# A decoder layer's feed-forward loop: a fifth chunk pair by Strassen's products, low parts by adding DMAs, seven slots

## The reference, cut to what matters

```python
f = rmsnorm(h, g_ffn)
h = h + (silu(f @ w_gate) * (f @ w_up)) @ w_down
```

## Time and profile before

| | |
|---|---|
| median of 3 runs | 1168.04 us (1167.95 to 1168.8) |
| the profiled execution | 1168.28 us, of which 1166.5 us are the span of the profile |
| PE, DVE, ACT, POOL busy | 1152.6, 944.9, 631.3, 141.5 us |
| granted TensorE clock | 0.998 of full speed |
| HBM read | 220.63 MB, 191 GB/s over the span |

### The profile page before, as it was taken

One profiled execution on the slowest core, in us unless ns is written; L12 is line 12 of the kernel. 1 busy time (PEld: TensorE's weight loads), 2 busy tenths in 40 slices (PEclk: granted clock), 3 DMA queues, 4 the chain that ended last, 5 costly groups with the idle time before them and its releaser, 6 DMA issues.

```text
span 1166.5 us, 16361 instructions
## 1 busy us (share of the span) xinstructions
PE 1152.6 (99%) x5618; PEld 969.2 (83%) x5618; DVE 944.9 (81%) x1266; ACT 631.3 (54%) x811; POOL 141.5 (12%) x90
## 2 busy tenths in 40 slices
PE   9999999999999999999999999999999999999996
PEld 8889989988888787888888888888888888888886
DVE  6589767767777999988989898988989898947674
ACT  6544365466465564646456564647364555637552
POOL 0212443336124300000000000000000000000111
PEclk9999999999999999999999999999999999999999
DMA  9655555444655575564747474745647374754541
GB/s 345 211 182 179 182 180 179 154 174 146 214 177 158 173 254 191 210 211 146 259 135 257 140 251 143 254 164 200 209 154 258 129 266 136 247 200 159 198 163 72
DMA packets 113120, 223.38 MB, mean 191 GB/s; under 512 B 5193, under 2 KB 6417, under 8 KB 112816
## 3 DMA queue, kind: packets, MB, share of 16 engines
q1 hardware_dynamic: 112608, 222.08, 56.2%
q10 hardware_dynamic: 464, 0.66, 0.2%
HBM read 220.63 MB, written 2.10 MB: 191 GB/s over the span
## 4 chain that ended last, share of the span: by engine, by line
PE 91%; DVE 3%; issue 2%; POOL 1%; ACT 1%; POOLq 0%; DVEq 0%; ACTq 0%
PE ps L1421 14%; PE ps L1423 14%; PE ps L1422 14%; PE ps L1624 12%; PE ps L1625 12%; PE ps L1626 12%; PE ps L1455 3%; PE ps L1454 3%; PE ps L1453 3%; PE ps L1463 2%; DVE w_lo L963 1%; PE ps L1619 1%; PE ps L1617 1%; PE ps L1618 1%; PE ps L1430 0%
## 5 line engine op out<-in xcount | busy, mean ns | idle before, releaser
L668 ACT ACTIVATE w_hi<-w_raw 128x1024 fp32r<-128x1024 f32 (+1 forms) x286 | 291.2, 1028 | 273.3 <-PE ps L1423 156.0
L963 DVE TENSOR_TENSOR w_lo<-w_raw,w_hi 128x1024 fp32r<-128x1024 f32 x250 | 301.9, 1220 | 121.0 <-ACT w_hi L668 120.7
L1421 PE MATMUL ps<-w_hi,oT_hi 128*128 128x512 f32 x320 | 125.8, 393 | 0.0
L1422 PE MATMUL ps<-w_lo,oT_hi 128*128 128x512 f32 x320 | 124.7, 390 | 0.0
L1423 PE MATMUL ps<-w_hi,oT_lo 128*128 128x512 f32 x320 | 124.7, 390 | 0.0
L1421 PE MATMUL ps<-w_hi,nT_hi 128*128 128x512 f32 x280 | 111.4, 398 | 0.0
L1423 PE MATMUL ps<-w_hi,nT_lo 128*128 128x512 f32 x280 | 109.1, 390 | 0.0
L1422 PE MATMUL ps<-w_lo,nT_hi 128*128 128x512 f32 x280 | 109.0, 389 | 0.0
L576 POOL TENSOR_TENSOR w_lo<-w_raw,w_hi 128x1024 fp32r<-128x1024 f32 x36 | 86.7, 2408 | 181.8 <-ACT w_hi L668 181.8
L1019 DVE SCALAR_TENSOR_TENSOR ps<-arena,taps,ps 128x256 f32<-128x256 f32 x232 | 94.6, 481 | 0.2 <-ACT ps L789 0.2
L1624 PE MATMUL ps<-w_hi,nT_hi 128*128 128x512 f32 x220 | 86.9, 395 | 1.4 <-DVE w_lo L963 1.4
(11 more groups left out here) (278 smaller groups left out, 2598.5 us busy)
## 6 DMA issues: line engine op xcount, KB each, us to landing
w_raw<-in_w_gate SPq DMA_DIRECT2D x88, 512.0 KB, 3.9
w_raw<-in_w_up SPq DMA_DIRECT2D x88, 512.0 KB, 4.8
w_raw<-in_w_down SPq DMA_DIRECT2D x44, 1024.0 KB, 5.1
w_raw<-in_w_in SPq DMA_DIRECT2D x32, 1024.0 KB, 5.1
w_raw<-in_w_out SPq DMA_DIRECT2D x16, 1024.0 KB, 5.0
w_raw<-in_w_pgate SPq DMA_DIRECT2D x16, 1024.0 KB, 5.1
w_raw<-in_w_in SPq DMA_DIRECT2D x14, 512.0 KB, 10.5
w_raw<-in_w_ple SPq DMA_DIRECT2D x2, 1024.0 KB, 7.4
```

Of the source, the lines that this page charges most:

```text
L668: nc.scalar.activation(tiles_of(m)[0], source_of(m), ACT.Copy).then_inc(hi_ready, 1)
L963: nc.vector.tensor_tensor(lo, source_of(m), hi.bitcast(F32), ALU.subtract).then_inc(lo_ready, 1)
L1421: nc.tensor.matmul(banks[t][:, :], x_hi[:, k, rows], hi[:, k], start=start, stop=False)
L1422: nc.tensor.matmul(banks[t][:, :], x_hi[:, k, rows], lo[:, k], start=False, stop=False)
```

## The change

- The kinds become PPSSSSSP: the fifth pair takes seven products too. A pass has 26 units of pairs and 8 of the down product, `PER_LOOP` = 34, `DOWN_AT` = 26.
- The fifth pair's sums of x take the rows of `oT_hi` and `oT_lo` that were a slot. Seven slots are left, and their numbering starts anew with each pass (`slot_back`). `align` moves ahead of `w_extra`.
- For the down columns 1, 2 and 3 DVE makes no low part. Behind the high part ACT writes a second `F32R` copy of the raw weights into the low tile, with `scale=-1.0`, and POOL issues a DMA that adds `w_down` from HBM to this tile (`accum_op=ALU.add`). SP reloads the raw buffer of such a column when this copy is done.
- The sums of x ahead of the loop move from POOL to DVE, two pairs in one instruction, and start one unit earlier; the first weight sums move behind the first swish.

```diff
-QUAD_KINDS = "PPSSPSSP"
+QUAD_KINDS = "PPSSSSSP"
-LOOP_SLOTS = 8
+LOOP_SLOTS = 7
+DMA_COLUMNS = (1, 2, 3)
-RB1_AT = FFN0 + 6
+RB1_AT = FFN0 + 5
-S_AT = {i: RB1_AT + 4 + n for n, i in enumerate(S_QUADS)}
+S_GROUPS = [S_QUADS[n:n + 2] for n in range(0, len(S_QUADS), 2)]
+X_SUMS_AT = [NORMAL_AT[group[-1]] for group in S_GROUPS]
+S_AT = [NORMAL_AT[group[-1]] + 1 for group in S_GROUPS]
...
+def by_dma(m):
+    return in_loop(m) and loop_unit(m)[0] == "D" and loop_unit(m)[1] in DMA_COLUMNS
...
+        sb("align", [P, 8])
         w_extra = sb("w_extra", [P, 2, 4, NP], F32R)
-        sb("align", [P, 8])
...
-                n = (m - LOOP0) % LOOP_SLOTS
+                n = (m - LOOP0) % PER_LOOP % LOOP_SLOTS
                 if n == 4:
-                    return tuple(o[:, 12:16].rearrange("p (k a) t -> p k (a t)", k=2) for o in (oT_hi, oT_lo))
-                if n == 5:
                     return w_more[:, 0:2], w_more[:, 2:4]
-                if n >= 6:
-                    return w_extra[:, n - 6, 0:2], w_extra[:, n - 6, 2:4]
+                if n > 4:
+                    return w_extra[:, n - 5, 0:2], w_extra[:, n - 5, 2:4]
                 return w_hi[:, n], w_lo[:, n]
...
+        def slot_back(m):
+            j = (m - LOOP0) % PER_LOOP
+            if j >= LOOP_SLOTS:
+                return LOOP_SLOTS
+            return PER_LOOP - max(k for k in range(PER_LOOP) if k % LOOP_SLOTS == j) + j
...
             elif in_loop(m) and m >= LOOP0 + LOOP_SLOTS:
-                engine.wait_ge(half_done, m - LOOP_SLOTS + 1 + PER_LOOP * it)
+                engine.wait_ge(half_done, m - slot_back(m) + 1 + PER_LOOP * it)
...
             def down_split(c, it):
+                if c in DMA_COLUMNS:
+                    sp.wait_ge(minus_hi_ready, 2 * (DMA_COLUMNS.index(c) + 1) + 2 * len(DMA_COLUMNS) * it)
+                    return
                 sp.wait_ge(lo_ready, lo_count(LOOP0 + DOWN_AT + 2 * c + 1, it))
...
-            for n, i in enumerate(S_QUADS):
-                x_sums(n, i)
+            done = 0
+            for m in filter(by_dma, range(LOOP0, PLE0)):
+                _, c, k = loop_unit(m)
+                rows = 4 * ((m - LOOP0) // PER_LOOP) + 2 * k
+                done += 1
+                pool.wait_ge(minus_hi_ready, done)
+                nc.gpsimd.dma_start(slot_of(m)[1], w_down_v[:, rows:rows + 2, c * NP:(c + 1) * NP], accum_op=ALU.add).then_inc(lo_by_dma[c, k], 16)
...
                 nc.scalar.activation(tiles_of(m)[0], source_of(m), ACT.Copy).then_inc(hi_ready, 1)
+                if by_dma(m):
+                    nc.scalar.activation(tiles_of(m)[1], source_of(m), ACT.Copy, scale=-1.0).then_inc(minus_hi_ready, 1)
...
             def split_lo(m, it=0):
+                if by_dma(m):
+                    return
...
+            def x_sums(g):
+                first, end = S_GROUPS[g][0], S_GROUPS[g][-1] + 1
+                x = w_sum[:, first:end].rearrange("p n (k t) -> p n k t", k=2)
+                a11, a12, a21, a22 = x[:, :, 0, 0:P], x[:, :, 1, 0:P], x[:, :, 0, P:T], x[:, :, 1, P:T]
+                out_s = s_raw(g)
+                ve.wait_ge(x_normal, end)
+                nc.vector.tensor_tensor(out_s[:, :, 0], a21, a22, ALU.add).then_inc(s_step, 1)
+                nc.vector.tensor_tensor(out_s[:, :, 2], a11, a21, ALU.subtract).then_inc(s_step, 1)
...
-                for i in S_QUADS:
-                    ahead = QUAD_AT[i] - LOOP_SLOTS
-                    if ahead < 0 and m - LOOP0 in (ahead, ahead + 1):
-                        weight_sums(m - LOOP0 - ahead, 0, i)
...
+                if m in (LOOP0 + SLOTS, LOOP0 + SLOTS + 1):
+                    weight_sums(m - LOOP0 - SLOTS, 0, S_FIRST)
                 split_lo(m)
...
             def arrived(m, it=0):
+                if by_dma(m):
+                    pe.wait_ge(hi_ready, m + 1 + PER_LOOP * it)
+                    pe.wait_ge(lo_by_dma[loop_unit(m)[1:]], 16 + 16 * it)
+                    return
                 pe.wait_ge(lo_ready_pool if by_pool(m) else lo_ready, lo_count(m, it))
```

More of the change, by code:

```diff
@@ L134, in by_pool @@
     return 8 <= m < POOL_UNTIL and (m % 4 == 3 or m % 2 == 1 and m >= POOL_HALF)
+def by_dma(m):
+    return in_loop(m) and loop_unit(m)[0] == "D" and loop_unit(m)[1] in DMA_COLUMNS
 def lo_count(m, it=0):
-    return sum(by_pool(i) == by_pool(m) for i in range(m + 1)) + PER_LOOP * it
+    return sum(by_pool(i) == by_pool(m) and not by_dma(i) for i in range(m + 1)) + (PER_LOOP - 2 * len(DMA_COLUMNS)) * it
 def taps_done(g, m):
@@ L270, in x_norm, with s_raw, s_parts @@
         def x_norm(i):
[L272 to L281, removed]
+            return w_sum[:, i].rearrange("p (k t) -> p k t", k=2)
+        def s_raw(g):
+            first = 2 * (g % 2)
+            return sums[:, first:first + len(S_GROUPS[g])].rearrange("p n (s t) -> p n s t", s=4)
+        def s_parts(n, count=1):
+            return tuple(o[:, 4 + 2 * n:4 + 2 * (n + count)].rearrange("p (n a) (b t) -> p n (a b) t", a=2, b=2)
+                         for o in (oT_hi, oT_lo))
         def a_parts(i):
@@ L374, in hybrid_decoder_layer @@
         w_sum_ready = sem("w_sum_ready")
+        minus_hi_ready = sem("minus_hi_ready")
+        lo_by_dma = {(c, k): sem(f"lo_by_dma{c}{k}") for c in DMA_COLUMNS for k in range(2)}
         x_joined, x_normal, s_step, s_hi_ready, s_ready = sem("x_joined"), sem("x_normal"), sem("s_step"), sem("s_hi_ready"), sem("s_ready")
@@ L583, in join_x @@
                                         ALU.add).then_inc(x_joined, 1)
[L585 to L597, removed]
             for m in filter(by_pool, range(POOL_UNTIL)):
@@ L856, in a_hi, with s_hi @@
                 nc.scalar.activation(a_parts(i)[0], x_norm(i), ACT.Copy).then_inc(a_hi_ready, 1)
-            def s_hi(n):
-                sc.wait_ge(s_step, 4 * n + 4)
-                nc.scalar.activation(s_parts(n)[0], s_raw(n), ACT.Copy).then_inc(s_hi_ready, 1)
+            def s_hi(g):
+                sc.wait_ge(s_step, 4 * g + 4)
+                nc.scalar.activation(s_parts(2 * g, len(S_GROUPS[g]))[0], s_raw(g), ACT.Copy).then_inc(s_hi_ready, 1)
             def sigmoid_gate(c):
@@ L876, in _ @@
                         a_hi(i)
-                for n, i in enumerate(S_QUADS):
-                    if m == S_AT[i]:
-                        s_hi(n)
+                for g in range(len(S_GROUPS)):
+                    if m == S_AT[g]:
+                        s_hi(g)
                 split_hi(m + AHEAD)
@@ L1217, in weight_sums @@
                         ve.wait_ge(a_ready, 4)
-                        ve.wait_ge(s_step, 4 * len([q for q in S_QUADS if q < 4]))
+                        ve.wait_ge(s_step, 4 * len([g for g in S_GROUPS if g[0] < 4]))
                     nc.vector.tensor_tensor(w_sum[:, 0:2], raw[:, 1:3], raw[:, 0:2], ALU.subtract).then_inc(w_sum_ready, 1)
@@ L1244, in _ @@
                         normalise(i)
+                for g in range(len(S_GROUPS)):
+                    if m == X_SUMS_AT[g]:
+                        x_sums(g)
                 if m == LOOP0 - 1:
@@ L1251, in _ @@
                         a_lo(i)
-                for n, i in enumerate(S_QUADS):
-                    if m == S_AT[i]:
-                        s_lo(n)
-                for i in S_QUADS:
-                    ahead = QUAD_AT[i] - LOOP_SLOTS
-                    if ahead < 0 and m - LOOP0 in (ahead, ahead + 1):
-                        weight_sums(m - LOOP0 - ahead, 0, i)
+                for g in range(len(S_GROUPS)):
+                    if m == S_AT[g]:
+                        s_lo(g)
                 if not by_pool(m + AHEAD) and m < LOOP0 - 1:
@@ L1640, in seven_products @@
                 s_hi, s_lo = s_parts(S_QUADS.index(i))
-                s1, s2, s3, s4 = ((s_hi[:, k], s_lo[:, k]) for k in range(4))
+                s1, s2, s3, s4 = ((s_hi[:, 0, k], s_lo[:, 0, k]) for k in range(4))
                 first, last = i == S_FIRST, i == S_LAST
                 pe.wait_ge(a_ready, i + 1)
-                pe.wait_ge(s_ready, S_QUADS.index(i) + 1)
+                pe.wait_ge(s_ready, S_QUADS.index(i) // 2 + 1)
                 arrived(at, it)
```

14 lines of the change are left out of this document (9 added, 5 removed).

## The result

The changed kernel takes 1258.14 us (median of 4 runs, 1257.44 to 1258.62) against 1168.25 for the kernel before in the same comparison: a ratio of 1.0767, 95% interval 1.075 to 1.0784. The forecast was 1217, its range 1186 to 1255. The direction was right and the size was not: 90 us more instead of 49, and 3 us beyond the range. TensorE's granted clock is 0.997 in the profiled execution and 0.998 in the one of before, so the clock has no part in this.

A forecast was written before the change was run, and what follows sets the result against it. TensorE, busy 99% of the span, bounds the kernel. A pass: 64.02 - 1.18 + 3 x 1.03 + 1.2 + 1.7 = 68.8 us; in all +48.8, so 1217 us, 4.2% slower, range 1186 to 1255.

The forecast's parts named there:

- fewer and closer matmuls: TensorE in each pass: three matmuls fewer (0.68 us) and 69 at aligned spacing (0.50 us), together 1.18 us saved.
- the pairs' waits: Five seven-product pairs in a row: TensorE waits for VectorE's late splits 0.17, 0.57 and 0.46, 1.2 us a pass.
- the first pass: First loop pass: VectorE, fuller and with later weight sums, is late; today's 1.65 us loss doubles, adding 1.6 us.
- ACT's copies of P1, P5: Before the first down column: ScalarE's copies queue behind eleven activations, are ready at 32.1, and TensorE waits 1.7 us a pass.
- three release waits a pass: End of pass: split and down-panel additions end 3.71 us after a 2.72 us unit began; TensorE waits 1.03 us, three times.
- adding DMAs: GpSimd's queue, down columns 1 to 3: each takes 9.6 us, just hidden under 10.3 or more, so they cost nothing.
- Engine time is no limit: DMA engines over a pass: six adding transfers, doubled, take 18.6 us on top of 37 in some 69, so they fit.
- Rival B: Adding DMAs late by slow descriptors or two fetches: first 5.0 us late each pass, 50 in all, 1267 us; chance 0.14.
- the alignment: Moving `align` ahead of `w_extra` brings 69 matmuls a pass from 0.2338 to 0.2265 us, saving 0.50 us a pass.
- Rival A: Only the end-of-pass waits occur; the 1.2 and 1.7 us margins in the pairs and ScalarE's queue vanish: 1188 us; chance 0.14.
- Rival C: Faster: the end-of-pass release chain takes below 2.72 us, no longer than a unit, and margins vanish: 1156 us; chance 0.09.
- The relief on DVE: Six low parts of 1.14 us leave VectorE at steps 21 to 26, where it is otherwise idle or combining: nothing gained in the pairs.

The follow-up runs named there:

- the kernels with GpSimd: Changed kernel without adding DMAs or copies by -1, additions early, GpSimd subtracting for six down units: 1186.38 us; also for one unit of three pairs: 1219.9 us.

## Why the prediction was right and wrong

The 90 us, each term by the runs that differ in it alone, beside the forecast's:

| term | forecast | measured | from |
|---|---|---|---|
| fewer and closer matmuls, the pairs' waits, the first pass | +1.8 | +8.4 | no DMAs, additions and copies earlier |
| ACT's copies of P1, P5 | +17 | +17.7 | copies earlier |
| three release waits a pass | +30 | +39.8 | additions earlier |
| adding DMAs | 0 | +24.0 | DMAs left out |
| sum | +49 | +89.9 | |

The measured terms add up in this order of removal; in another the shares of the last two would differ, as the run with the DMAs in place and the additions earlier shows.

**The step that failed** is "Engine time is no limit: ... six a pass, doubled, are 18.6 us on top of 37 in some 69". Its terms were good: an adding transfer takes 2.87 us of the 16 engines against 1.67 plain, 1.72 times, six of them 17.2 us. What was wrong is the 69. The six fall into one third of the pass, and SP's loads for the next pass fall into the same third. The queues of the window over the six units in the kernel after show both (packets, MB, share of 16 engines):

```profile
q0 software_dynamic: 1318, 2.53, 65.0%
q1 hardware_dynamic: 1653, 3.18, 44.3%
```

109% together, over 21 us. The kernel without the adding DMAs shows the room that there was, in the 12 us ahead of the stage and in the stage:

```profile
643.00:655.00 12.00, 10.52 (x47) 8.40 (x46) 7.66 (x11) 12.00 (x15) 0.00 (x0) 1.00 0.87 315
655.00:671.50 16.50, 14.20 (x62) 11.13 (x61) 9.68 (x12) 6.07 (x7) 0.00 (x0) 1.00 0.50 167
```

Half of 16.5 us and 0.13 of 12 are some 10 us of engine time, and 17 came. With the engines full, the first transfer of a pass (second to ninth) lands some 9.4 us after its issue, within the 9.6 taken, but the others after 11.3 to 13.8, each 4.0 us behind the one ahead. Rival B, DMAs late at 1267, had the place, the sign and the point from which it decides (10.3 us), and was given 0.14. It erred in the form: it charged one lateness of 5.0 us a pass, but what comes is a rate. The first DMA is in time, and the five behind it are each late, 0.8 to 1.3 us at a time, 5.5 in a pass; and since PE is then held anyway, the release waits vanish into it. A pass gets 1.8 us longer by the DMAs (72.3 against 70.5), the first one 3.9, and the last stretch 5.5: there the two loads of `w_ple` stand behind adding DMAs, land in 11.3 us, ACT waits 6.65 for them, and PE 5.20 behind ACT and DVE. 8 x 1.83 + 3.9 + 5.5 make the 24.0. That last wait was in no step.

The Trainium skill (Collectives: The Full Stack, The bandwidth ceiling) has two sources read where there is a reduction, and so half the rate; the runs show 1.72 times the engine time. The Trainium skill's fit (DMA: Bandwidth & Descriptors, Anatomy of one DMA) gives 3.2 us for one such transfer by itself; among the others it took 8.9 plain and 11.7 adding. The nearest to a transfer by itself is the first one of the last pass, beside which SP's loads run out 2.5 us after its issue: it lands in 5.7 us adding and in 4.4 plain, so here the measurement is above the fit.

**A term mis-sized:** the release wait. Mechanism, places and number of waits were as forecast (28 of 29; all three go when the additions move). Its price was taken from the earlier trace rows at 1.03 us; it is 1.41. Of the 0.38 between, 0.09 is the chain on ACT and DVE, 0.18 the two further waits that PE passes before it starts and 0.11 the late second matmul behind it. The same 0.11 makes the pairs' three waits 1.34 + 0.33 = 1.67 us where the forecast has 1.2, and this 0.47, ten times, is most of the 6.6 us by which the first line of the table is off. The first pass is the rest: without DMAs and with both moved it is 4.7 us over the others (69.29 against 64.55), where 1.65 + 1.6 was taken.

**Right:** the waits inside the pairs (0.57, 0.44 and 0.33 against 0.17, 0.57 and 0.46), in all 1.34 for 1.2; ACT's late copies (1.64 against 1.7); the alignment, 5.2 us measured for 5.0; no change ahead of the loop; the passes without DMAs 70.5 against 68.8. **Rival A** (these margins vanish) fell: both waits are there, within 0.15 us of their sizes. **Rival C** (faster) fell: the chain is 4.02, not below 2.72. The relief on DVE was said to give nothing back, and it does not: with the additions early DVE makes all low parts at no cost. GpSimd's 60 issues took 1.2 us each (one 1.36), so nothing held it while it wrote descriptors.

Four things stay open. Why the first pass waits more: its timeline shows DVE behind in every pair, with three waits of 0.8 and eight of 0.2 to 0.4 where a later pass has three in all, but no run changed the order ahead of it. The adding DMA's 1.72 is measured at one size of packet and from HBM to SBUF only. No run moved SP's loads out of the stage, so that the adding DMAs would be in time without them is argued from the last pass alone. And the kernels with GpSimd show that contended operations stand still, but only 6.2 of the 9 us of the first are seen as waits of PE.

## What to carry to other kernels

Work out engine time of DMAs over the stage in which they are issued, with what the other queues load in that stage, not over the pass; a queue that loads ahead is at its fullest just where its buffers come free. Before moving work to an engine or a queue "that has nothing else to do", look whether the one relieved was late at all: here, without the DMAs, the order of the down additions and of two copies cost 57 us, and DVE's six low parts nothing. Remember that causes can cover each other: what one edit gives back holds only beside the edits it was measured with. And where a wait is worked out as chain minus cover, add what the restart costs: here a chain 7% longer than read and one late matmul made the wait a third longer.

## What the runs showed of the hardware

- An adding DMA of 512 KB from HBM into SBUF took 2.87 us of all 16 engines, a plain one of the same shape 1.67; with the engines full, 272 against 375 GB/s. Adding transfers landed 4.0 us apart beside SP's loads and 2.97 apart without them.
- A `tensor_tensor` of DVE with both inputs in SBUF stood still for the 2.22 us that a GpSimd subtraction still had to run: 3.30 us for 1.23. With one input in PSUM it kept its 0.7 us.
- Matmuls of 512 columns followed each other by 0.2338 us from a tile that lies 32 bytes off the alignment of the others, and by 0.2267 when the filler was moved: 3% for 32 bytes.
- After a wait PE's second matmul came 0.31 to 0.34 us behind the first instead of 0.23. The first came 0.05 us after the end of what released it where PE had one wait to pass, 0.13 with two, 0.22 with three.
